# The modulation of two conditioned blocks, moved from matrix products on TensorE to row sums on VectorE

## The chip, the cores and the metric

The kernel runs on one core of one Trainium2 chip. The metric is device time in microseconds, one launch from start to end. Engines are named as the profile names them: PE (TensorE), DVE (VectorE), ACT (ScalarE), POOL (GpSimd), SP (SyncE, which here only issues transfers).

## The reference

A first block (feed-forward, a mixer, feed-forward) works on 256 tokens of width 1024. Then two conditioned layers work on these tokens and on 256 context tokens. All matrices are float32. In each layer a vector of 9 x 1024 numbers, the modulation, is worked out from a condition vector, once for the tokens (`c`) and once for the context (`c_ctx`):

```python
mod = jax.nn.silu(c) @ w_ada[l] + b_ada[l]            # 1024 x 9216, l = 0, 1
modc = jax.nn.silu(c_ctx) @ w_ada[l] + b_ada[l]
def ada_norm(h, g, shift, scale):
    return rms_norm_2(h, g) * (1 + scale) + shift
h = h + HALF * gt1 * swiglu_2(ada_norm(h, g_ffn1[l], sh1, sc1), w1_ffn1[l], w3_ffn1[l], w2_ffn1[l])
u = ada_norm(h, g_mix[l], sh2, sc2)                   # then attention, convolution, Fourier branch
h = h + gt2 * y
h = h + HALF * gt3 * swiglu_2(ada_norm(h, g_ffn2[l], sh3, sc3), w1_ffn2[l], w3_ffn2[l], w2_ffn2[l])
```

A third of the modulation (3 x 1024 numbers) belongs to each of the three parts of a layer. `w_ada` is 37.7 MB per layer, 144 pieces of 512 KB for both.

## The kernel before

**Stages.** In order: f1 (feed-forward, 256 columns), mix1 (gated delta and banded attention), f2 (256 columns), then layer 0 with 512 columns (f10, mix of layer 0, f20) and layer 1 (f11 with 512 columns, mix of layer 1, f21 with 256).

**Weights.** All weights lie in one stream in HBM, cut into units of at most 128 x 1024 numbers (512 KB). SP loads them in order into the ring `w_raw` of NR = 4 slots (line 2201). Before the load of unit u it waits until unit u - 4 is done with: for an ordinary unit until its `w_lo` exists, for a unit of the modulation until its product is over (line 2199). An ordinary unit is split into two halves for fp32r products: ACT writes `w_hi` (line 1520), DVE writes `w_lo` = raw - hi (line 1753), into rings of NH = 3. TensorE then runs three products per 128 x 128 piece (lines 1220 to 1222). So a unit of 8 pieces is 24 matmuls, called a gemm here.

**Order.** `Plan` writes one list of steps, and every engine works through its own steps of that list in order. `with_splits` (line 203) puts the split of a unit AHEAD = 2 units before the step that uses unit u, that is: before the gemm of u stands the split of u + 2.

**Feed-forward** (`ffn`, line 342). For j = 0 to 21: gemm g, gemm u, then the step `ffn_h`: ACT silu (1552), DVE product (1792), ACT high half (1555), DVE low half (1794). One such j is called a turn below. Then for m = 0 to 7 a down gemm of 22 pieces (3 units) and `x_add` (1804), with squares for the next norm.

**Modulation.** A step `ada` is one unit (two pieces of 128 x 512): TensorE multiplies it, with the four columns of `CSIL` as the stationary operand, into a bank of 4 x 512 (line 1259, unsplit float32, two instructions per piece). Four steps make a bank, ACT copies it (1559), four small transposes (1269) turn it and DVE adds the bias (1817, 1819). The 144 steps stand where `FILL` says: beside the norms between stages, beside the attention heads and the delta rule of mix1, beside the latents and heads of the mixes of layers 0 and 1 (42 and 18), and 20 in f11 in split form (1261, 1262). `derive` (line 296) turns a third of the modulation into the factors of the next norm (1824 to 1828).

**Other transfers.** POOL issues the constants of the mixes (lines 2146 to 2185).

The two lines that set when a slot of the raw ring is refilled:

```python
if u >= NR:
    w.wait_ge(*(used(u - NR) if plan.raw_only(u - NR) else at("w_lo", u - NR)))
```

Of the kernel before, what the change touches and what calls it, by code (L numbers as in the profile page):

```python
# [163 lines left out]
class Plan:  # L164


    def __init__(self):
# [4 lines left out]
        self.adas = iter([(l, m, k) for l in range(2) for m in range(18) for k in range(0, 8, 2)])
        self.todo, self.split_ada, self.bank, self.summed, self.rows = 0, False, None, [], []
        self.mod_done, self.count = None, 0
        self.whole()
# [24 lines left out]
    def raw_only(self, u):  # L200
        return self.units[u][2][0][0][0][:3] == "adr"

    def with_splits(self):

        steps, cuts, used, nxt, top = [], [], set(), 0, 0
        self.slot, self.over = {}, {}
        for s in self.steps:
# [4 lines left out]
            else:  # L212
                turns = sorted({wt[0] for wt in s.wts})
            for u in turns:
                if s.wts:
# [1 line left out]
                if s.kind != "ahead":
                    top = max(top, u)
                while nxt < min(u + AHEAD + 1, len(self.units)) and (
                        self.raw_only(nxt) or len(cuts) < NH or cuts[-NH] in used):  # L220
                    if not self.raw_only(nxt):
                        self.slot[nxt] = len(cuts) % NH
                        self.over[nxt] = cuts[-NH] if len(cuts) >= NH else None
                        cuts.append(nxt)
                        steps.append(Step("split", u=nxt))
                    nxt += 1
# [28 lines left out]
    def advance(self):  # L255

        if self.rows:
            l, m, t = self.rows.pop(0)
            b = self.PS.get()
            self.add("ada_col", key=(l, m), b=b, t=t)  # L260
            self.TM.done(t, ("ada_tr", (l, m)))
            self.PS.done(b, ("mod", (l, m)))
            self.mod_done = ("mod", (l, m))
        if self.summed:
            l, m, b = self.summed.pop(0)
            t = self.TM.get()
            self.add("ada_row", key=(l, m), b=b, t=t)
            self.PS.done(b, ("ada_row", (l, m)))
            self.rows.append((l, m, t))

    def fill(self, most=1000):

        while most and self.todo:
            most -= 1
            self.todo -= 1
            l, m, k = next(self.adas)
            self.bank = self.bank or self.PS.get()
            name = f"{'ada' if self.split_ada else 'adr'}{l}"
            wts = self.weights([(name, i, 512 * m, 512) for i in (k, k + 1)])
            self.add("ada", key=(l, m, k), wts=wts, b=self.bank)  # L280
            self.count += 1
            if k == 6:
                self.summed.append((l, m, self.bank))
                self.bank = None

    def due(self, n):
        self.todo += n

    def ada_steps(self, n):
        for _ in range(n):  # L290
            self.due(1)
            self.advance()
            self.fill(1)
            yield

    def derive(self, l, i):
        while any((l_, m) < (l, 6 * (i + 1)) for l_, m, *_ in self.rows + self.summed):
            self.advance()
        assert self.count >= 72 * l + 24 * (i + 1)
        self.add("derive", key=(l, i), need=(self.mod_done,))  # L300

    def stat(self, name, n):
        self.late = None
        return Stat(self, name, n)
# [37 lines left out]
    def ffn(self, p, n, wts, need, gate, old):  # L342
        for j in range(NF):
            if j == 0:
                g, u = self.pair([(p, "g", 0), (p, "u", 0)], wts, n, need)
            else:
                if j <= FILL.get(f"in_{p}", 0):
                    self.split_ada = True
                    self.due(1)
# [20 lines left out]
    def whole(self):  # L370
# [10 lines left out]
        rb = stat.rsqrt(D, between=FILL["mix1"])  # L381
# [14 lines left out]
        rb = stat.rsqrt(D, between=FILL["f10"] // 2)  # L396
# [5 lines left out]
    def block2(self, wts):  # L402
# [4 lines left out]
        for l in range(2):  # L407
# [4 lines left out]
            rb = stat.rsqrt(D, between=FILL["f11"] if l else FILL["f10"] - FILL["f10"] // 2)  # L412
# [1891 lines left out]
```

## Time and profile before

| | |
|---|---|
| time, median of 3 runs (lowest, highest) | 3089.04 us (3087.8, 3096.08) |
| the profiled execution: its time, its span | 3089.18 us, 3087.3 us |
| mean granted clock of TensorE | 0.978 |
| busy: PE, DVE, ACT, POOL | 2929.6, 1464.7, 1073.5, 49.6 us |
| read from HBM | 376.36 MB |
| f10, f20 (512 columns) | 368.4 us each |
| f1, f2 (256 columns) | 184.6, 185.7 us |
| f11 (with 20 split modulation steps) | 388.7 us |
| mix1; mix of layer 0; of layer 1 | 352.6; 573.9; 343.3 us |

The stages are read from the first and last matmul of each. An engine that is busy for a small share of the span can still be the one that a stage waits for; the rows below show the order of events inside a stage. A matmul's duration contains pipelining, so the distance from start to start says more than the duration.

### The profile page before, as it was taken

Reading aid. Unit: us, or ns where it says so; the run is one execution under the profiler, and the core shown is the slowest. Engines: PE = TensorE matmul, PEld = TensorE weight load, DVE = VectorE, ACT = ScalarE, POOL = GpSimd, SP = SyncE. Lnnn points to the kernel's source line nnn. Section 1 sums busy time; section 2 is a strip of 40 time slices with the busy share of each in tenths; the row PEclk is TensorE's granted clock in tenths of the full one; section 3 lists DMA queues with packets and bytes.
Section 4 is the critical chain, followed back from the end, with each engine's and each line's share of the span. In section 5 each row is a group of like instructions: output and inputs, shape, how many; then the busy total and the mean of one; then the engine's idle time right before and its main releaser. Section 6 shows DMA issues by size and latency. Waiting matters only on the chain.

```text
span 3087.3 us, 38316 instructions
## 1 busy us (share of the span) xinstructions
PE 2929.6 (95%) x15892; PEld 2318.7 (75%) x15892; DVE 1464.7 (47%) x2293; ACT 1073.5 (35%) x1630; POOL 49.6 (2%) x49
## 2 busy tenths in 40 slices
PE   8998999999899999988999999999999999879998
PEld 7988457899688885434888788886777866569898
DVE  5556454565433334476333533334444334656664
ACT  5445312444322222233222322223333223335543
POOL 0010022000000000000000000000000000000000
PEclk9999999999999999989999999999999999989999
DMA  6654331555222233422232323323434234215464
GB/s 211 191 206 144 116 103 31 183 196 186 96 96 92 93 97 126 144 78 88 75 96 92 113 90 96 93 94 115 129 124 134 94 125 132 97 51 189 167 194 144
DMA packets 110348, 379.91 MB, mean 123 GB/s; under 512 B 12064, under 2 KB 17440, under 8 KB 109920
## 3 DMA queue, kind: packets, MB, share of 16 engines
q1 hardware_dynamic: 109360, 372.28, 37.4%
q0 software_dynamic: 816, 5.18, 0.5%
q8 instruction: 127, 2.08, 0.3%
q14 instruction: 45, 0.37, 0.0%
HBM read 376.36 MB, written 1.05 MB: 122 GB/s over the span
## 4 chain that ended last, share of the span: by engine, by line
PE 88%; DVE 6%; ACT 3%; DMA 1%; issue 1%; SPq 0%; DVEq 0%; ACTq 0%
PE B L1220 24%; PE B L1221 23%; PE B L1222 23%; PE B L1259 5%; PE B L1457 2%; DMA w_raw<-in_w 1%; DVE w_lo L1753 1%; ACT w_hi L1520 1%; PE B L1235 1%; DVE AC L2012 1%; PE B L1473 1%; PE B L1237 1%; PE B L1236 1%; PE B L1381 1%; PE B L1367 1%
## 5 line engine op out<-in xcount | busy, mean ns | idle before, releaser
L1753 DVE TENSOR_TENSOR w_lo<-w_raw,w_hi 128x1024 fp32r<-128x1024 f32 (+3 forms) x611 | 717.8, 1179 | 851.6 <-ACT w_hi L1520 851.3
L1220 PE MATMUL B<-UH,w_hi 128*128 128x256 f32 (+1 forms) x2896 | 970.5, 335 | 20.4 <-DVE w_lo L1753 18.0
L1221 PE MATMUL B<-UL,w_hi 128*128 128x256 f32 (+1 forms) x2896 | 963.3, 333 | 0.0
L1222 PE MATMUL B<-UH,w_lo 128*128 128x256 f32 (+1 forms) x2896 | 963.0, 333 | 0.0
L1520 ACT ACTIVATE w_hi<-w_raw 128x1024 fp32r<-128x1024 f32 (+3 forms) x611 | 613.1, 1008 | 580.1 <-PE B L1222 531.7
L1220 PEld LDWEIGHTS B<-UH,w_hi 128*128 128x128 f32 x2896 | 547.9, 189 | 95.8 <-issue 21.3
L1221 PEld LDWEIGHTS B<-UL,w_hi 128*128 128x128 f32 x2896 | 547.8, 189 | 62.0 <-issue 1.3
L1222 PEld LDWEIGHTS B<-UH,w_lo 128*128 128x128 f32 x2896 | 547.8, 189 | 61.1
L1220 PE MATMUL B<-HHf,w_hi 128*128 128x256 f32 (+1 forms) x1056 | 354.8, 336 | 0.0
L1221 PE MATMUL B<-HLf,w_hi 128*128 128x256 f32 (+1 forms) x1056 | 354.8, 336 | 0.0
L1222 PE MATMUL B<-HHf,w_lo 128*128 128x256 f32 (+1 forms) x1056 | 354.8, 336 | 0.0
L1259 PE MATMUL B<-w_raw,CSIL 128*4 128x512 f32 x496 | 235.6, 614 | 5.7 <-ACT TMP L1559 5.7
L1555 ACT ACTIVATE HHf<-TMP 128x256 fp32r<-128x256 f32 (+1 forms) x132 | 69.4, 526 | 423.3 <-DVE TMP L1792 423.3
L1220 PEld LDWEIGHTS B<-HHf,w_hi 128*128 128x128 f32 x1056 | 200.4, 190 | 20.8
L1222 PEld LDWEIGHTS B<-HHf,w_lo 128*128 128x128 f32 x1056 | 200.4, 190 | 20.6
L1221 PEld LDWEIGHTS B<-HLf,w_hi 128*128 128x128 f32 x1056 | 200.4, 190 | 20.4
L1792 DVE TENSOR_TENSOR TMP<-TMP,B 128x256 f32<-128x256 f32 (+1 forms) x132 | 73.2, 554 | 238.2 <-PE B L1222 234.6
L1259 PEld LDWEIGHTS B<-w_raw,CSIL 128*4 128x4 f32 x496 | 37.3, 87 | 156.1 <-issue 146.3
L1794 DVE TENSOR_TENSOR HLf<-TMP,HHf 128x256 fp32r<-128x256 f32 (+1 forms) x132 | 73.7, 559 | 78.2 <-ACT HHf L1555 78.2
L2012 DVE SCALAR_TENSOR_TENSOR AC<-VC,PC,AC 128x512 f32<-128x512 f32 (+1 forms) x180 | 99.3, 609 | 0.1
L1525 ACT ACTIVATE TMP<-X 128x256 f32<-128x256 f32 (+1 forms) x77 | 38.3, 512 | 171.0 <-DVE X L1804 136.9
L1457 PE MATMUL B<-QK 96*128 96x512 f32 (+1 forms) x96 | 51.5, 683 | 24.1 <-DVE QK L2064 24.1
(362 smaller groups left out, 2515.7 us busy)
## 6 DMA issues: line engine op xcount, KB each, us to landing
w_raw<-in_w SPq DMA_DIRECT2D x636, 512.0 KB, 3.5
w_raw<-in_w SPq DMA_DIRECT2D x50, 384.0 KB, 3.1
w_raw<-in_w SPq DMA_DIRECT2D x16, 448.0 KB, 4.1
w_raw<-in_w SPq DMA_DIRECT2D x16, 256.0 KB, 2.6
w_raw<-in_w SPq DMA_DIRECT2D x16, 240.0 KB, 2.6
X<-in_x SPq DMA_DIRECT2D x2, 1024.0 KB, 8.7
BW<-in_bias POOLq DMA_DIRECT2D x1, 1536.0 KB, 11.8
K<-in_consts POOLq DMA_DIRECT2D x2, 640.0 KB, 4.8
```

The lines of the kernel that those rows point to most:

```text
L1220: pe.matmul(o, hi, xh, start=i == 0, stop=False)
L1221: pe.matmul(o, hi, xl, start=False, stop=False)
L1222: e = pe.matmul(o, lo, xh, start=False, stop=i == last)
L1259: e = pe.matmul(PS(s.b, 512, 4), CSIL[:, i, :], hi, start=i == 0, stop=i == 7)
L1457: pe.matmul(PS(s.b, nk), QK[:, s.q.i, qs:qs + 128], QK[:, 3 + s.kk.i, k0:k0 + nk], start=True, stop=True).then_inc(*up("soft_s", s.key))
L1520: act.activation(w_hi[:, plan.slot[u], 0:n], w_raw[:, u % NR, 0:n], ACT.Copy).then_inc(*up("w_hi", u))
L1525: act.activation(TM(s.t, s.n), src(s), ACT.Square).then_inc(*up("sq", s.key))
L1555: act.activation(HI[p][:, j, :], TM(s.t, s.n), ACT.Copy).then_inc(*up("hh", s.key))
L1753: dve.tensor_tensor(w_lo[:, plan.slot[u], 0:n], w_raw[:, u % NR, 0:n], w_hi[:, plan.slot[u], 0:n].bitcast(F32), ALU.subtract).then_inc(*up ...
L1792: dve.tensor_tensor(h, h, PS(s.b2, s.n), ALU.mult).then_inc(*up("hm", s.key))
L1794: dve.tensor_tensor(LO[p][:, j, :], h, HI[p][:, j, :].bitcast(F32), ALU.subtract).then_inc(*up("hl", s.key))
L2012: dve.scalar_tensor_tensor(out=AC[:, c], in0=VC[:, c, :, i:i + 256], scalar=col(f"w_dw{l}", 31 * c + i), in1=AC[:, c], op0=ALU.mult, op1=A ...
```

## The change

The modulation is worked out by DVE. The host lays out `w_ada` transposed, so that a unit `adt` is 128 outputs (partitions) by 1024 inputs. Each of 144 steps `ada` is two multiply-and-sum instructions over such a raw unit, one with silu(c), one with silu(c_ctx), which lie as rows repeated over all partitions in `CS` (1 MB, loaded and put through silu at the start). The steps stand only in the feed-forward stages, after `ffn_h` of turns 1 to 21 and after `x_add` of each m: 12, 12, 48, 48 and 24 of them in f1, f2, f10, f20 and f11, spread evenly over the 29 places. All other places of `FILL`, the TensorE products, the copies and transposes go. The bias is added in `derive`. `with_splits` counts only the ordinary units when it looks ahead. The constants of the mixes are issued by ACT and no longer by POOL. NR, NH and AHEAD stay.

```diff
+ADA = {"f1": 12, "f2": 12, "f10": 48, "f20": 48, "f11": 24, "f21": 0}
...
     def with_splits(self):
+        cut = [u for u in range(len(self.units)) if not self.raw_only(u)]
+        place = {u: i for i, u in enumerate(cut)}
...
-                turns = sorted({wt[0] for wt in s.wts})
+                turns = sorted({wt[0] for wt in s.wts} & place.keys())
...
+                at = place[u] if u in place else place[top] + 1
+                while done < min(at + AHEAD + 1, len(cut)) and (done < NH or cut[done - NH] in used):
+                    steps.append(Step("split", u=cut[done]))
+                    done += 1
...
     def gemm(self, key, pieces, n, m=128, x="U", need=(), wts=None):
-        self.advance()
-        self.fill()
...
+    def ada(self, n):
+        for l, b in [next(self.adas) for _ in range(n)]:
+            self.add("ada", key=(l, b), wts=self.weights([(f"adt{l}", b, 0, 1024)]))
+            self.last_ada = (l, b)
...
     def ffn(self, p, n, wts, need, gate, old):
+        turns, share = 0, lambda i: i * ADA[p] // (NF + 7)
...
             self.TM.done(t, ("hl", (p, j)))
+            if j:
+                self.ada(share(turns + 1) - share(turns))
+                turns += 1
...
             stat.add_("X", m, ("x_add", (p, m)))
+            self.ada(share(turns + 1) - share(turns))
+            turns += 1
...
             if k == "load":
+                w.wait_ge(*at("cvec", 0))
+                act.activation(CS[:], CS[:], ACT.Silu).then_inc(*up("cs", 0))
+            elif k == "mix1_load":
+                w.each(s.need)
+                act.dma_start(CN[:], consts[:, 256:2560]).then_inc(*landed("cn", 0))
...
+            if k == "ada":
+                (l, b), u = s.key, s.wts[0][0]
+                raw = w_raw[:, u % NR, :]
+                w.wait_ge(*at(f"w{u % NR}", u))
+                w.wait_ge(*at("cs", 0))
...
+                dve.tensor_tensor_reduce(JUNK[:], raw, CS[:, 0, :], 1.0, 0.0, ALU.mult, ALU.add,
+                                         MOD[:, l, b, 0:1]).then_inc(*up("ada_x", s.key))
+                dve.tensor_tensor_reduce(raw, raw, CS[:, 1, :], 1.0, 0.0, ALU.mult, ALU.add,
+                                         MOD[:, l, b, 1:2]).then_inc(*up("ada", s.key, ("unit", u)))
...
             elif k == "derive":
-                w.each(s.need)
+                mod, bias = MOD[:, l, 24 * i:24 * i + 24, :], col(f"b_ada{l}", 24 * i, 24)
+                w.wait_ge(*at("ada", (l, 24 * i + 23)))
+                dve.tensor_tensor(mod, mod, bias.unsqueeze(2).broadcast_to([128, 24, 2]), ALU.add).then_inc(*up("mod", s.key))
...
         sp.dma_start(C1[:], consts[:, 0:256]).then_inc(*landed("c1", 0))
+        sp.dma_start(CS[:].rearrange("p v k -> p (v k)"), bass.AP(tensor=cvec.tensor, offset=0, ap=[[0, 128], [1, 2048]])).then_inc(
+            *landed("cvec", 0))
```

## Rows read from the trace of the kernel before

**Rows 1.** The page: the chain that ended last, share of the span by line.

```profile
PE B L1220 24%; PE B L1221 23%; PE B L1222 23%; PE B L1259 5%; PE B L1457 2%; DMA w_raw<-in_w 1%; DVE w_lo L1753 1%; ACT w_hi L1520 1%; PE B L1235 1%; DVE AC L2012 1%; PE B L1473 1%; PE B L1237 1%; PE B L1236 1%; PE B L1381 1%; PE B L1367 1%
```

**Rows 2.** Windows: stretch and length, busy time (instructions) by engine, clock, DMA.

```profile
17.40:202.00 184.60, 184.59 (x1584) 184.39 (x1584) 106.87 (x136) 89.52 (x126) 0.00 (x0) 1.00 0.58 187
789.40:1157.80 368.40, 368.39 (x1592) 297.50 (x1592) 130.06 (x160) 104.40 (x134) 0.00 (x0) 1.00 0.29 94
1157.80:1170.40 12.60, 9.23 (x22) 1.86 (x21) 5.57 (x14) 4.62 (x8) 0.90 (x3) 1.00 0.58 188
...
2138.30:2527.00 388.70, 388.66 (x1688) 305.03 (x1688) 153.68 (x188) 125.23 (x158) 0.00 (x0) 1.00 0.37 117
...
2884.00:2892.00 8.00, 1.75 (x5) 0.98 (x5) 5.07 (x11) 5.34 (x9) 0.00 (x0) 0.72 0.57 193
```

**Rows 3.** Chain of waits in 333:396, 396:528, 528:567, 1273:1300, 1300:1450, by line.

```profile
by line: PE B L1259 57.0%; PE B L1309 13.4%; PE B L1326 12.8%; PE B L1317 7.5%; PE B L1291 2.9%; PE B L1269 2.7%; PE B L1339 1.7%; ACT TMP L1559 0.9%; issue 0.8%; PE B L1342 0.7%; ACT PT L1626 0.0%
...
by line: PE B L1381 16.3%; PE B L1367 15.4%; PE B L1374 13.9%; PE B L1259 12.3%; DVE GDN L1955 3.6%; DVE GDN L1953 3.6%; DVE GDN L1957 3.0%; PE B L1396 2.9%; PE B L1351 2.9%; PE B L1355 2.9%; PE B L1412 2.7%; PE B L1342 2.6%; DVE GDN L1959 
...
by line: PE B L1259 22.2%; ACT w_hi L1520 21.4%; issue 20.6%; DMA w_raw<-in_w 12.8%; DVE w_lo L1753 9.9%; DVE X L1810 8.0%; PE B L1419 2.9%; PE B L1246 2.0%; ACT TMP L1559 1.5%; DVE SSB L1760 0.9%; ACT TMP L1525 0.4%; ACTq L1031 0.3%; ACT S
...
by line: PE B L1259 77.7%; PE B L1220 6.6%; PE B L1221 5.1%; PE B L1222 5.1%; PE B L1269 3.7%; PE B L1448 1.6%; PE B L1440 0.9%
...
by line: PE B L1259 20.2%; PE B L1457 18.3%; PE B L1473 10.5%; DVE AC L2012 7.6%; PE B L1464 6.3%; PE B L1220 4.5%; PE B L1221 4.5%; PE B L1222 4.5%; ACT TMP L1697 3.0%; PE B L1448 2.8%; DVE QK L2064 2.3%; DVE TMP L2060 2.1%; DVE w_lo L1753
```

**Rows 4.** Windows over the part of layer 0's mix that holds the convolution's taps.

```profile
1226.00:1450.00 224.00, 198.43 (x692) 92.96 (x690) 139.15 (x302) 59.73 (x136) 0.00 (x0) 0.95 0.35 114
```

**Rows 5.** Timeline of DVE, one turn of f10: start, length [idle before, releaser].

```profile
881.43 0.69 DVE L1792 TENSOR_TENSOR TMP<-TMP,B 128x512 f32<-128x512 f32 x1 [3.29 <-PE B L1222]
882.82 0.69 DVE L1794 TENSOR_TENSOR HLf<-TMP,HHf 128x512 fp32r<-128x512 f32 x1 [0.70 <-ACT HHf L1555]
883.77 1.23 DVE L1753 TENSOR_TENSOR w_lo<-w_raw,w_hi 128x1024 fp32r<-128x1024 f32 x1 [0.26 <-ACT w_hi L1520]
888.11 1.23 DVE L1753 TENSOR_TENSOR w_lo<-w_raw,w_hi 128x1024 fp32r<-128x1024 f32 x1 [3.12 <-ACT w_hi L1520]
892.63 0.69 DVE L1792 TENSOR_TENSOR TMP<-TMP,B 128x512 f32<-128x512 f32 x1 [3.29 <-PE B L1222]
```

**Rows 6.** Timeline of ACT in the same turn.

```profile
882.69 1.04 ACT L1520 ACTIVATE w_hi<-w_raw 128x1024 fp32r<-128x1024 f32 x1
```

**Rows 7.** DMA issues of 790:1160, us to landing; the page's queues, MB and share.

```profile
w_raw<-in_w SPq DMA_DIRECT2D x59, 512.0 KB, 3.3
...
q1 hardware_dynamic: 109360, 372.28, 37.4%
```

**Rows 8.** Timeline of DVE: sums of products in the banded attention of mix1.

```profile
345.40 0.43 DVE L1907 CUSTOM_DVE_ANT_0 TMP<-TMP,CB 128x256 f32<-128x256 f32 x1
345.75 0.08 DVE L1907 DVE_READ_ACCUMULATOR2_ANT SMALL<- 128x1 f32 x1
345.75 0.42 DVE L1907 CUSTOM_DVE_ANT_0 TMP<-TMP,CB 128x256 f32<-128x256 f32 x1
```

**Rows 9.** Timeline of DVE, one turn of f1.

```profile
100.68 0.42 DVE L1792 TENSOR_TENSOR TMP<-TMP,B 128x256 f32<-128x256 f32 x1 [0.41 <-PE B L1222]
101.59 0.43 DVE L1794 TENSOR_TENSOR HLf<-TMP,HHf 128x256 fp32r<-128x256 f32 x1 [0.48 <-ACT HHf L1555]
102.54 1.22 DVE L1753 TENSOR_TENSOR w_lo<-w_raw,w_hi 128x1024 fp32r<-128x1024 f32 x1 [0.52 <-ACT w_hi L1520]
...
106.12 0.42 DVE L1792 TENSOR_TENSOR TMP<-TMP,B 128x256 f32<-128x256 f32 x1 [0.41 <-PE B L1222]
```

**Rows 10.** Timeline of PE, a wait in mix1; and the window after it (clock 0.50).

```profile
223.38 0.55 PE L1220 MATMUL B<-UH,w_hi 128*128 128x256 f32 x1 [3.87 <-DVE w_lo L1753]
...
221.70:228.40 6.70, 5.02 (x23) 5.05 (x24) 5.64 (x9) 1.09 (x3) 0.45 (x1) 0.50 0.50 157
```

**Rows 11.** Chain of waits at the start: start, us, what.

```profile
1.46 6.43 DMA PC<-in_cols
8.68 2.14 ACT TMP L1525 x7
```

More of the change, by code:

```diff
@@ L171, in __init__ @@
         self.nid, self.lastU = 0, None
-        self.adas = iter([(l, m, k) for l in range(2) for m in range(18) for k in range(0, 8, 2)])
-        self.todo, self.split_ada, self.bank, self.summed, self.rows = 0, False, None, [], []
-        self.mod_done, self.count = None, 0
+        self.adas = iter([(l, b) for l in range(2) for b in range(72)])
+        self.last_ada = None
         self.whole()
@@ L200, in raw_only @@
     def raw_only(self, u):
-        return self.units[u][2][0][0][0][:3] == "adr"
+        return self.units[u][2][0][0][0][:3] == "adt"
     def with_splits(self):
-        steps, cuts, used, nxt, top = [], [], set(), 0, 0
-        self.slot, self.over = {}, {}
+        cut = [u for u in range(len(self.units)) if not self.raw_only(u)]
+        place = {u: i for i, u in enumerate(cut)}
+        steps, used, done, top = [], set(), 0, 0
+        self.slot = {u: i % NH for u, i in place.items()}
+        self.over = {u: cut[i - NH] if i >= NH else None for u, i in place.items()}
         for s in self.steps:
@@ L216, in with_splits @@
                     used |= {v for v in turns if v < u}
[L217 to L226, printed above, removed]
+                at = place[u] if u in place else place[top] + 1
+                top = max(top, u) if s.kind != "ahead" else top
+                while done < min(at + AHEAD + 1, len(cut)) and (done < NH or cut[done - NH] in used):
+                    steps.append(Step("split", u=cut[done]))
+                    done += 1
             if s.kind not in ("fetch", "ahead"):
@@ L253, in pair @@
         return b, b2
[L255 to L294, printed above, removed]
-    def derive(self, l, i):
[L297 to L304, printed above, removed]
+    def ada(self, n):
+        for l, b in [next(self.adas) for _ in range(n)]:
+            self.add("ada", key=(l, b), wts=self.weights([(f"adt{l}", b, 0, 1024)]))
+            self.last_ada = (l, b)
+    def derive(self, l, i):
+        assert self.last_ada >= (l, 24 * i + 23)
+        self.add("derive", key=(l, i))
     def norm_to_u(self, name, rb, wait_u):
@@ L380, in whole @@
         wts = self.fetch([("win", k, 128 * j, 128) for k in range(8) for j in range(2)])
-        rb = stat.rsqrt(D, between=FILL["mix1"])
+        rb = stat.rsqrt(D)
         need = self.norm_to_u("mix_norm", rb, self.lastU)
@@ L395, in whole @@
         wts = self.fetch(self.first_of("f10"))
-        rb = stat.rsqrt(D, between=FILL["f10"] // 2)
+        rb = stat.rsqrt(D)
         for k in range(8):
@@ L411, in block2 @@
             self.derive(l, 0)
-            rb = stat.rsqrt(D, between=FILL["f11"] if l else FILL["f10"] - FILL["f10"] // 2)
+            rb = stat.rsqrt(D)
             need = self.ada_to_u(f"n1{l}", l, 0, rb, 512, self.lastU)
@@ L585, in mix1 @@
         tasks += [band(c) for c in range(4)]
-        def later(n):
-            while len(qn) < 8:
-                yield
-            yield from self.ada_steps(n)
-        beside(rounds(tasks, WIDTH1, 1), later(FILL["swa"]))
+        for _ in rounds(tasks, WIDTH1, 1):
+            pass
         first_o = {}
@@ L670, in delta @@
             PS.done(b, ("dl_os", key))
-        beside(rounds([delta(o, d) for o in range(2) for d in range(2)], 4), self.ada_steps(FILL["gdn"] - 5))
-        self.due(5)
+        for _ in rounds([delta(o, d) for o in range(2) for d in range(2)], 4):
+            pass
         def finish(c):
@@ L781, in prep @@
                 q, kk = QR.get(), KR.get()
-                for _ in range(FILL[f"head{l}"]):
-                    self.due(1)
-                    self.advance()
-                    self.fill(1)
-                    yield
                 yield from PS.room(3)
@@ L961, in settle, with rsqrt @@
             self.p.TM.done(self.late, ("sq_add", (self.name, self.i - 1)))
-    def rsqrt(self, count, ring=None, between=0):
+    def rsqrt(self, count, ring=None):
         p = self.p
@@ L1555, in scalar @@
                 act.activation(HI[p][:, j, :], TM(s.t, s.n), ACT.Copy).then_inc(*up("hh", s.key))
-            elif k == "ada_row":
-                w.wait_ge(*at("ada", (*s.key, 6)))
-                w.each(s.t.after)
-                act.activation(TM(s.t, 512, 4), PS(s.b, 512, 4), ACT.Copy).then_inc(*up("ada_row", s.key))
             elif k == "conv_in":
```

111 lines of the change are left out of this document (28 added, 83 removed).

## The prediction

> **What bounds the kernel now.** I read the page's chain first. TensorE products hold nearly all of it, and line 1259, the modulation, is 5% of the span [rows 1]. The windows by stage come next: in the feed-forward stages TensorE never stands still, 184.59 busy in 184.60 us in f1 and 368.39 in 368.40 in f10, while VectorE is busy 106.87 and 130.06 us [rows 2]. By shares alone VectorE has room for the new work. So I looked at how the chain runs in the mixes [rows 3, 4], and then at the order of events in one turn [rows 5, 6, 9] with the loads [rows 7], because every new step also holds a slot of the raw ring until VectorE is through with it.
>
> **What is removed.** Shares of the chain times their stretches give what line 1259 holds on it in the mixes [rows 3]: attention of mix1 0.57 x 63 = 36 us, delta rule 0.123 x 132 = 16, before the out projection 0.222 x 39 = 8.7 with 0.128 x 39 = 5.0 of a refilled raw ring behind it, layer 0 0.777 x 27 = 21 and 0.202 x 150 = 30. Not all of it comes back, for there it fills TensorE while VectorE and ScalarE work.
> - Mix1: of the 36 us of attention I take 27 (six steps at its end stand alone, 11 us; the other 25 us lie between short round trips), of the 16 of the delta rule 10, of 8.7 + 5.0 I take 10, since the out projection still waits for its input. Together 47.
> - Layer 0: from 1226 to 1450 us VectorE is busy 139 of 224 us [rows 4]. If it stays busy at most four fifths of the time, this takes 174 us, 50 less. The taps are dealt out one batch per round of the attention, and rounds that held only modulation vanish, so more taps come alone at the end. I take 45. Bounds are 25 and 56 (the whole chain share, with 3.6 us beside the latents). Layer 1 has 18 steps instead of 42; I take 12.
> - f11 carried 20 split steps: 388.70 against 368.40 us [rows 2], 20 us.
> - The transitions. One with no modulation, 256 columns, takes 8.00 us, one with four steps, 512 columns, 12.60 [rows 2]. After f10 and f20 I take nothing: two new steps stand on VectorE behind the last x_add (4.8 us, below), the third ordinary unit waits for the slot of the first of them, and its split stands ahead of the norm; release, load 3.3, halves 1.04 and 1.23 end at about the old time. Elsewhere: into mix1 2, into f2 6, into f10 8 (six steps were there), into f20 5, into the mix of layer 1 4. Together 25.
> In all 47 + 45 + 12 + 20 + 25 = 149 us less. Bounds: 105 (half of the mixes and transitions, 65, the whole of f11, and the ring's refill and layer 0's far stretch in part, 20) and 185 (every share in full).
>
> **What a new step costs VectorE.** The trace has the same kind of instruction with 256 columns, 0.42 us and 0.35 from start to start, and an ordinary one of 256 columns takes 0.42 too [rows 8, 9]. So 1024 columns take what `w_lo` takes, 1.23 us [rows 5], about 1.2 from start to start, and a step of two takes 2.4 us. As work it is nothing: 48 steps are 115 us beside 130 in 368. The DVE Microarchitecture Reference of the Trainium skill, section "Points that are easy to get wrong", says that a sum over two SBUF sources that aren't bf16 runs at half rate; line 1907 reads two such sources and doesn't [rows 8]; by the rule its pitch would be 0.7, and a step near 4.8 us.
>
> **What a new step costs the ring.** Take a turn of f10. Let 0 be the end of gemm u. VectorE then runs the product and the low half until 2.1 us (881.43 to 883.5), and then `w_lo` of the unit due next [rows 5]. The new steps stand between the two. With a steps, they end at D = 2.1 + 2.4a. With two steps in the next turn the ring of four holds g, u and two steps, so the second new load, g and u can all be issued only at D: the slot before each is the last step's, or stands behind it in SP's queue. A load alone lands 3.3 us after its issue, and further ones 1.5 us apart (372 MB in 37.4% of the span is 322 GB/s, 1.6 us for 512 KB at full use [rows 7]). With two steps, g lands at D + 4.7 and u at D + 6.2; `w_hi` takes 1.04 [rows 6], `w_lo` 1.23 with 0.05 between; u is ready at D + 8.55. In VectorE's order `w_lo` of u stands ahead of the next product, so the next D is 8.55 + 2.1 + 4.8 = 15.45 us later. TensorE needs 11.2 for a turn (881.43 to 892.63 [rows 5]). With one step in the next turn nothing stands ahead of g: 7.05 + 2.1 + 2.4 = 11.55. Of the 21 turns 13 have two steps and 8 have one: 13 x 15.45 + 8 x 11.55 = 293 us against 235, 58 more, less 1 for the start. In the down part (8 turns of 15.35 us) the loads need about 15 us and I take 3. What waits behind the blocked SP queue is the weight of the next turn, and for it TensorE, up to 4.2 us per turn.
> Such gaps cost clock as well: after a wait of 3.87 us the granted clock was 0.50 for 6.7 us [rows 10], which is 1.2 instead of 2.4 GHz. Inside a turn of 15.45 there is room for the 3 us lost, in one of 11.55 there isn't; I take 3 per stage. So f10 and f20 cost 63 each, 126. Bounds for one: 35 (loads land 1 us earlier and 1.0 apart, step 2.2) and 95 (step 2.6, clock low in most turns). The Trainium skill, TensorE: Matmul & The Clock Gate, section "HAM oscillation", describes a loop whose products are shorter than its wait for data and that starts cold each time; here the products are the longer part, so by it too only a part of each turn would be cold.
> f1 and f2: a turn is 5.44 us and has at most one step, 8 in turns and 4 in the down part [rows 9]. D = 1.4 + 2.4 = 3.8. Only u two gemms on waits for the slot: landed 7.1, ready 9.45, due 8.16, so TensorE waits 1.3, and 0.3 to 1 more in the next turn, since VectorE starts its product late. 8 x 1.9 + 4 x 1.4 = 21 each, 42 for both. Bounds 15 and 70. f11: turns of at most one step, 11.55 against 11.2, with four empty turns to recover: 3.
>
> **The rest.** At the start the condition rows (1 MB) stand in SP's queue ahead of the weights, and ACT's silu of 2048 columns (2 x 1.04) waits for them ahead of the squares, which start at 8.68 [rows 11]: 4 us, bounds 0 and 7. The constants move from POOL's queue to ACT's behind the norm: three issues in mix1, hidden beside the norm, 0, bounds -2 and +4. `derive` gains one small instruction, three of six under a longer wait: 0.
>
> **Sum.** 3089.2 (the profiled execution, whose span is 3087.3; the median shown is 3089.0) - 149 + 126 + 42 + 3 + 4 = 3115 us.
>
> **Rivals.**
> 1. The ring stalls as I say, but TensorE is the limit in the mixes, and they give back the whole share: 185 instead of 149, and with the stalls at the lower third (160 instead of 175) 3089 - 185 + 160 = 3064. For it: TensorE is busy 198 of 224 us in [rows 4]. Against: 139 us of VectorE there. It decides where the mixes give back more than the feed-forward stages lose, 175. Chance 0.17.
> 2. The steps hide in the feed-forward stages: the loads come early enough, as VectorE's idle share suggests [rows 2]. Then 3089 - 149 + 4 = 2944. Against: D stands ahead of the load by the order of the units. Chance 0.05.
> 3. The clock falls in each stalled turn of f10 and f20 and TensorE becomes late in turns of one step too: 3 us x 16 turns more, 3163 us. For it [rows 10]. Chance 0.13.
> 4. The sums run at half rate. A step takes 4.8: 13 x 4.8 + 8 x 2.4 = 82 more in each of f10 and f20, some 2.2 us x 24 in f1 and f2: 3332. Against [rows 8]. Chance 0.03.
> My forecast has 0.62.
>
> **How the numbers follow.** A measurement here can't tell less than about 0.3% (9 us) from no change. Between 3080 and 3098 lies about 0.15, taken from the lower side of the forecast and the upper of rival 1. Faster: rivals 1 and 2 less a part, and the lowest of the forecast, 0.2. Slower 0.65. The range is 3065 to 3170: below it rival 2 and half of rival 1, above it rival 4 and a part of rival 3.
>
> **What would show it.** Right: f10 and f20 last about 430 us, TensorE waits there for `w_lo` 3 to 4 us in turns of two steps, ScalarE's `w_hi` waits for the transfer and no longer for TensorE, VectorE's sums take about 1.2 us; f1 and f2 last about 205; layer 0's mix about 530, mix1 about 305; f11 371. Wrong: f10 at 368 (the ring has slack I missed), sums of 2.3 us, or mixes that shorten by less than half of the share of line 1259.

## The result and the profile after

| | before | after |
|---|---|---|
| time, median (lowest, highest), 4 runs each | 3090.53 us (3087.8, 3096.08) | 3105.67 us (3101.86, 3106.81) |
| span of the profiled execution | 3087.3 us | 3100.1 us |
| mean granted clock | 0.978 | 0.946 |

The ratio is 1.0037, interval 1.0023 to 1.0051: slower by 0.4%, which is 11 us by the ratio, 13 by the two profiled executions and 15 by the medians. The forecast was 26 us: the sign came true, about half of the size. The span splits up as follows; a stage begins with the first matmul behind its norm and ends with its last matmul. Forecast terms are those of the prediction, with the transition into f2 and into f20 added to the mix ahead of it.

| stretch | before | after | difference | forecast |
|---|---|---|---|---|
| start of f1 | 17.4 | 21.7 | +4.3 | +4 |
| f1 | 184.6 | 214.5 | +29.9 | +21 |
| to mix1 | 8.7 | 5.8 | -2.9 | -2 |
| mix1, to the start of f2 | 366.7 | 326.8 | -39.9 | -53 |
| f2 | 185.7 | 216.1 | +30.4 | +21 |
| to f10 | 26.3 | 21.2 | -5.1 | -8 |
| f10 | 368.5 | 422.4 | +53.9 | +63 |
| to the mix of layer 0 | 12.6 | 13.5 | +0.9 | 0 |
| mix of layer 0, to the start of f20 | 586.7 | 522.2 | -64.5 | -50 |
| f20 | 368.4 | 426.2 | +57.8 | +63 |
| to f11 | 12.8 | 14.0 | +1.2 | 0 |
| f11 | 388.7 | 367.7 | -21.0 | -17 |
| to the mix of layer 1 | 13.7 | 8.3 | -5.4 | -4 |
| mix of layer 1, to the start of f21 | 351.3 | 318.2 | -33.1 | -12 |
| f21 | 186.0 | 192.0 | +6.0 | 0 |

So 170 us came back (forecast 146) and 182 were paid (forecast 172).

The page of the kernel after: busy time by engine, then the chain that ended last, by engine and by line.

```profile
PE 2747.9 (89%) x15172; PEld 2339.4 (75%) x15172; DVE 1746.8 (56%) x2782; ACT 1043.7 (34%) x1573; POOL 44.7 (1%) x41
...
PE 52%; DVE 20%; DMA 13%; ACT 7%; issue 6%; SPq 1%; DVEq 0%; ACTq 0%
PE B L1155 13%; PE B L1157 13%; PE B L1156 13%; DMA w_raw<-in_w 13%; DVE JUNK L1671 4%; ACT w_hi L1442 4%; DVE w_lo L1678 3%; DVE w_raw L1673 3%; DVE AC L1932 2%; DVE TMP L1717 1%; PE B L1371 1%; ACT HHf L1477 1%; PE B L1170 1%; PE B L1171 1%; PE B L1172 1%
```

Against [rows 1]: before, TensorE held 88% of the chain, now it holds half. The line of the page before:

```profile
PE 88%; DVE 6%; ACT 3%; DMA 1%; issue 1%; SPq 0%; DVEq 0%; ACTq 0%
```

Now transfers hold 13%, VectorE 20%. The same in the page's groups (count, busy time and mean ns of one, then the idle time before them and what ended it):

```profile
L1442 ACT ACTIVATE w_hi<-w_raw 128x1024 fp32r<-128x1024 f32 (+3 forms) x591 | 593.9, 1008 | 997.7 <-DMA w_raw<-in_w 811.8
...
L1673 DVE CUSTOM_DVE_ANT_0 w_raw<-w_raw,CS 128x1024 f32<-128x1024 f32 x144 | 175.6, 1219 | 0.0
L1671 DVE CUSTOM_DVE_ANT_0 JUNK<-w_raw,CS 128x1024 f32<-128x1024 f32 x144 | 175.4, 1218 | 0.0
...
w_raw<-in_w SPq DMA_DIRECT2D x636, 512.0 KB, 3.9
```

288 sums at 1.22 us: the price of the instruction is as forecast, and so is what `w_hi` waits for. The window of f10, with f1 ahead of it (columns as in [rows 2]):

```profile
21.70:236.20 214.50, 197.64 (x1584) 194.08 (x1584) 129.32 (x180) 89.21 (x126) 0.00 (x0) 0.99 0.53 185
806.10:1228.50 422.40, 379.34 (x1584) 306.30 (x1584) 231.19 (x340) 106.04 (x132) 0.00 (x0) 0.96 0.38 136
2204.40:2572.10 367.70, 364.38 (x1584) 298.07 (x1584) 179.90 (x249) 104.81 (x132) 0.00 (x0) 0.99 0.35 123
```

In f10 TensorE was busy 368.39 of 368.40 us [rows 2]; now it stands still 43 us, VectorE is busy 231 of 422, and the granted clock is 0.96. One turn of VectorE in f10, start, length, idle before, as [rows 5]:

```profile
884.89 0.68 DVE L1717 TENSOR_TENSOR TMP<-TMP,B 128x512 f32<-128x512 f32 x1
886.27 0.69 DVE L1719 TENSOR_TENSOR HLf<-TMP,HHf 128x512 fp32r<-128x512 f32 x1 [0.69 <-ACT HHf L1477]
886.88 1.22 DVE L1671 CUSTOM_DVE_ANT_0 JUNK<-w_raw,CS 128x1024 f32<-128x1024 f32 x1
...
888.02 1.22 DVE L1673 CUSTOM_DVE_ANT_0 w_raw<-w_raw,CS 128x1024 f32<-128x1024 f32 x1
...
889.17 1.22 DVE L1671 CUSTOM_DVE_ANT_0 JUNK<-w_raw,CS 128x1024 f32<-128x1024 f32 x1
...
890.31 1.22 DVE L1673 CUSTOM_DVE_ANT_0 w_raw<-w_raw,CS 128x1024 f32<-128x1024 f32 x1
...
896.47 2.45 DVE L1678 TENSOR_TENSOR w_lo<-w_raw,w_hi 128x1024 fp32r<-128x1024 f32 x2 [4.93 <-ACT w_hi L1442]
898.84 0.68 DVE L1717 TENSOR_TENSOR TMP<-TMP,B 128x512 f32<-128x512 f32 x1
...
911.60 0.68 DVE L1717 TENSOR_TENSOR TMP<-TMP,B 128x512 f32<-128x512 f32 x1
...
913.59 1.22 DVE L1671 CUSTOM_DVE_ANT_0 JUNK<-w_raw,CS 128x1024 f32<-128x1024 f32 x1
```

Two steps stand on VectorE from 886.88 to 891.5. Then it waits 4.93 us, not for lack of work but for ScalarE's `w_hi`, and that waits for the transfer (ACT, same turn):

```profile
883.63 0.58 ACT L1474 ACTIVATE TMP<-B 128x512 f32<-128x512 f32 x1
...
895.38 1.06 ACT L1442 ACTIVATE w_hi<-w_raw 128x1024 fp32r<-128x1024 f32 x1 [9.14 <-DMA w_raw<-in_w]
896.61 1.06 ACT L1442 ACTIVATE w_hi<-w_raw 128x1024 fp32r<-128x1024 f32 x1 [0.17 <-DMA w_raw<-in_w]
...
907.93 1.06 ACT L1442 ACTIVATE w_hi<-w_raw 128x1024 fp32r<-128x1024 f32 x1 [7.75 <-DMA w_raw<-in_w]
```

The four loads behind these steps were issued at 889.28, 891.57, 891.94 and 892.42 and landed at 892.51, 895.36, 896.58 and 897.82: 3.2 us for the first; the last three, issued within 0.9 us, landed 1.2 us apart (1.2 to 1.5 in the next two turns). The same wait, over the whole kernel (engine, line, what it waited for: total, times, longest):

```profile
ACT w_hi L1442 <- DMA w_raw<-in_w: 811.8, 209, 10.8
...
ACT w_hi L1442 <- PE B L1157: 160.2, 95, 4.4
PE B L1155 <- DVE w_lo L1678: 131.6, 78, 8.3
```

Before, it was the other way round:

```profile
ACT w_hi L1520 <- PE B L1222: 531.7, 231, 4.4
...
ACT w_hi L1520 <- DMA w_raw<-in_w: 31.5, 19, 4.9
```

### The profile page after: what moved, and what is told of

Its sections match the earlier page's. It is cut to its first block, busy times and chain, and to the rows that moved or that the text cites. A ratio compares the mean times of both kernels' runs of the same rounds, so it can differ in the third digit from the quotient of the medians.

```text
span 3100.1 us, 37377 instructions
## 1 busy us (share of the span) xinstructions
PE 2747.9 (89%) x15172; PEld 2339.4 (75%) x15172; DVE 1746.8 (56%) x2782; ACT 1043.7 (34%) x1573; POOL 44.7 (1%) x41
## 4 chain that ended last, share of the span: by engine, by line
PE 52%; DVE 20%; DMA 13%; ACT 7%; issue 6%; SPq 1%; DVEq 0%; ACTq 0%
PE B L1155 13%; PE B L1157 13%; PE B L1156 13%; DMA w_raw<-in_w 13%; DVE JUNK L1671 4%; ACT w_hi L1442 4%; DVE w_lo L1678 3%; DVE w_raw L1673 3%; DVE AC L1932 2%; DVE TMP L1717 1%; PE B L1371 1%; ACT HHf L1477 1%; PE B L1170 1%; PE B L1171 1%; PE B L1172 1%
## 5 line engine op out<-in xcount | busy, mean ns | idle before, releaser
L1678 DVE TENSOR_TENSOR w_lo<-w_raw,w_hi 128x1024 fp32r<-128x1024 f32 (+3 forms) x591 | 688.1, 1167 | 918.9 <-ACT w_hi L1442 916.5
L1155 PE MATMUL B<-UH,w_hi 128*128 128x256 f32 (+1 forms) x2896 | 992.0, 343 | 123.5 <-DVE w_lo L1678 119.5
L1156 PE MATMUL B<-UL,w_hi 128*128 128x256 f32 (+1 forms) x2896 | 977.9, 338 | 0.0
L1157 PE MATMUL B<-UH,w_lo 128*128 128x256 f32 (+1 forms) x2896 | 976.9, 337 | 0.0
L1442 ACT ACTIVATE w_hi<-w_raw 128x1024 fp32r<-128x1024 f32 (+3 forms) x591 | 593.9, 1008 | 997.7 <-DMA w_raw<-in_w 811.8
L1155 PEld LDWEIGHTS B<-UH,w_hi 128*128 128x128 f32 x2896 | 562.3, 194 | 204.3 <-issue 148.2
L1156 PEld LDWEIGHTS B<-UL,w_hi 128*128 128x128 f32 x2896 | 562.5, 194 | 55.7 <-issue 2.3
L1157 PEld LDWEIGHTS B<-UH,w_lo 128*128 128x128 f32 x2896 | 561.8, 194 | 55.6
L1673 DVE CUSTOM_DVE_ANT_0 w_raw<-w_raw,CS 128x1024 f32<-128x1024 f32 x144 | 175.6, 1219 | 0.0
L1671 DVE CUSTOM_DVE_ANT_0 JUNK<-w_raw,CS 128x1024 f32<-128x1024 f32 x144 | 175.4, 1218 | 0.0
L1170 PE MATMUL B<-UH,w_hi 128*128 128x256 f32 (+1 forms) x144 | 57.6, 400 | 46.1 <-DVE UL L1709 36.9
L1717 DVE TENSOR_TENSOR TMP<-TMP,B 128x256 f32<-128x256 f32 (+1 forms) x132 | 72.5, 549 | 43.7 <-PE B L1157 41.6
```

Source lines behind the costliest of these rows:

```text
L1155: pe.matmul(o, hi, xh, start=i == 0, stop=False)
L1156: pe.matmul(o, hi, xl, start=False, stop=False)
L1157: e = pe.matmul(o, lo, xh, start=False, stop=i == last)
L1170: pe.matmul(o, hi, UH[:, k, 0:s.n], start=k == 0, stop=False)
L1442: act.activation(w_hi[:, plan.slot[u], 0:n], w_raw[:, u % NR, 0:n], ACT.Copy).then_inc(*up("w_hi", u))
L1671: dve.tensor_tensor_reduce(JUNK[:], raw, CS[:, 0, :], 1.0, 0.0, ALU.mult, ALU.add, MOD[:, l, b, 0:1]).then_inc(*up("ada_x", s.key))
```

## The experiments

Times of single runs are good to about 0.3%; the kernels that leave out a part of the modulation's work ran once each. Where a ratio is given, it is to the kernel before on the same chip, whose medians were 3087.3 to 3090.5 us in all groups of runs.

**Is it the ring?** For the 60 us in f10 and f20 my theory was the ring (R in the texts on record): each step holds a slot and so delays the loads behind it. Its rivals were VectorE's own time, which delays the splits, and the transfers, since more bytes cross the same stretch. Six slots or five, with the throwaway output of the sums moved into space that is free in the feed-forward stages, and a smaller scratch for transfers to make room (not shown):

```diff
-NR, NH, AHEAD = 4, 3, 2
+NR, NH, AHEAD = 6, 3, 2
-    CS, JUNK = sb("CS", [128, 2, 1024]), sb("JUNK", [128, 1024])
+    CS = sb("CS", [128, 2, 1024])
...
+            if ADA[p]:
+                if n == 256:
+                    sb("PAD" + p, [128, 11264], F32, st)
+                JK[p] = sb("JUNK" + p, [128, 1024], F32, st)
```

> The changed kernel with six slots in the raw ring instead of four (the scratch output of the sums moves to space that is free in the feed-forward stages). Theory R, the ring: a step keeps its slot until VectorE is through with it, and with six slots the next turn's g waits only for the first step of a turn and lands in time; f10 and f20 fall from 422 and 426 us to 370 to 378, f1 and f2 from 215 to 186 to 192, the whole to about 2945 us. Rival V, VectorE's order: the 4.8 us of sums stand ahead of the halves whatever the ring is; f10 and f20 stay above 410 and the whole above 3080. Rival M, the transfers of these stages interfere: the same as V.

> The same with five slots. Theory R: between the two; in turns of two steps g still stands behind the release of the second step or just before it, so about a half to three quarters of the loss goes: f10 and f20 at 380 to 400 us, f1 and f2 at 190 to 200, the whole at 2970 to 3030. Rivals V and M: no less than 3080.

Six slots: 2924.35 us, ratio 0.9475 (0.9454 to 0.9495), f10 361.7, f20 364.3, f1 191.9, f2 191.5 us. That is below the 370 to 378 us expected for f10 and f20, for a reason that comes further down, the place of the operands. Five: 2995.68 us, 0.9711 (0.9686 to 0.9737), f10 390.8, f20 398.0, f1 195.5. With six slots `w_hi` waits for the transfer less than half as long:

```profile
ACT w_hi L1448 <- DMA w_raw<-in_w: 346.5, 94, 7.7
ACT w_hi L1448 <- PE B L1163: 339.9, 179, 4.7
```

Next, the sums over 8 columns in place of 1024 (slots and loads kept), and the full sums without their loads and slots:

```diff
-                dve.tensor_tensor_reduce(JUNK[:], raw, CS[:, 0, :], 1.0, 0.0, ALU.mult, ALU.add,
+                dve.tensor_tensor_reduce(JUNK[:, 0:8], raw[:, 0:8], CS[:, 0, 0:8], 1.0, 0.0, ALU.mult, ALU.add,
```

```diff
-            self.add("ada", key=(l, b), wts=self.weights([(f"adt{l}", b, 0, 1024)]))
+            self.add("ada", key=(l, b))
...
-                dve.tensor_tensor_reduce(JUNK[:], raw, CS[:, 0, :], 1.0, 0.0, ALU.mult, ALU.add,
+                dve.tensor_tensor_reduce(JUNK[:], CS[:, 1, :], CS[:, 0, :], 1.0, 0.0, ALU.mult, ALU.add,
```

> The changed kernel with sums over 8 columns instead of 1024 (the modulation isn't the reference's); loads, slots, waits and their order stay. Theory R: release comes 2.2 us per step earlier, the loop of two steps is 15 - 4.4 = 10.6 us and under TensorE's 11.2, so f10 is 368 to 374 us and f1 and f2 are 186 to 192. Rival M: f10 stays over 410, since the traffic is the same. V expects the same as R here.

> The changed kernel with the sums of full length over the condition rows alone; the transposed weights are neither loaded nor given a slot (the modulation isn't the reference's). Theory R: VectorE's work alone hides; f10 is 368 to 374 us, f1 and f2 185 to 190. Rival V: f10 stays over 400 and f1 over 205, since the halves stand behind the same sums.

Short sums: 2949.69 us, f10 377.5, f20 371.1, f1 194.2. Full sums without loads: 2912.51 us, f10 360.8, f20 360.9, f1 191.6. So VectorE's 2.4 us per step cost nothing by themselves: with all 288 sums in place f10 runs at full speed when no slot is tied to them. They cost only through the slot that they hold, and most of that goes when the hold is short. Not all: with short sums f10 is still 17 us above the stage without loads, and over the 374 us expected at most; a slot is held until VectorE comes to the step, however short the step is. The bytes aren't it either: with six slots the same bytes cross in a shorter time. The theory of the ring stands, the two others fall.

**Where did more come back than forecast?** The mixes of layers 0 and 1 gave back 97.6 us, forecast 62, the transition into f20 in it. From the kernel before, without any modulation; and with its products 128 columns wide in place of 512 (the units are still loaded and hold slots):

```diff
-            wts = self.weights([(name, i, 512 * m, 512) for i in (k, k + 1)])
-            self.add("ada", key=(l, m, k), wts=wts, b=self.bank)
...
-        self.add("derive", key=(l, i), need=(self.mod_done,))
+        self.add("derive", key=(l, i))
...
+                pool.memset(MOD[:], 0.0).then_inc(*up("mod_zero", 0))
```

```diff
-                        e = pe.matmul(PS(s.b, 512, 4), CSIL[:, i, :], hi, start=i == 0, stop=i == 7)
+                        e = pe.matmul(PS(s.b, 128, 4), CSIL[:, i, :], hi[:, 0:128], start=i == 0, stop=i == 7)
```

> The kernel before with no modulation at all (set to zero): no units, no products, no copies and transposes. It has neither cost, so it gives what the mixes and transitions give back in full, in the layout and with the queues of before. Theory P and L both: layer 1 at 315 to 320 us, layer 0 at 520 to 530, mix1 at 320 to 327, f10, f20 and f11 at 368. If the mixes stay above that, a part of the gain of the changed kernel came from something else in the change (the queue of the constants, the count of the look-ahead).

> The kernel before, with each TensorE product of the modulation 128 columns wide instead of 512 (the modulation isn't the reference's); its units, their loads and their slots stay. Asked is what the mixes gave back: from the start of the mix of layer 1 to f21 the changed kernel took 318 us instead of 351, from the mix of layer 0 to f20 522 instead of 587, from mix1 to f2 327 instead of 367. Theory P: it is TensorE's time, so here most of it comes back too: layer 1 at 323 to 330, layer 0 at 535 to 545, mix1 at 330 to 340. Theory L: it is what the units do to the loads, whose slots they hold until TensorE reaches them; then layer 1 stays above 335 us and its first attention product stays 75 to 86 us behind the start of the mix (before 86, after 58).

Then the opposite: full-width products over a constant, with no units loaded (in f11 they ran unsplit for that, so f11, 408.7 us, is not compared); and the kernel before with six slots.

```diff
-            wts = self.weights([(name, i, 512 * m, 512) for i in (k, k + 1)])
-            self.add("ada", key=(l, m, k), wts=wts, b=self.bank)
+            self.add("ada", key=(l, m, k), b=self.bank)
...
+                    e = pe.matmul(PS(s.b, 512, 4).rearrange('p (a b) -> p a b', a=4), CSIL[:, i, :], C1[:, 0:128].unsqueeze(1).broadcast_to([128, 4, 128]), start=i == 0, stop=i == 7)
```

> The kernel before with TensorE's products of the modulation kept in number and width, but over a constant in SBUF; their units are neither loaded nor given a slot (the modulation isn't the reference's). The complement of the run with narrow products, which left layer 1's mix at 351 us and layer 0's at 577. Theory L, the units' hold on the raw ring and the look-ahead cost the time of these two mixes: layer 1 is 320 to 330 us and layer 0 530 to 550, although TensorE has all its products. Theory P: they stay above 345 and 575. In mix1, where narrow products gave 37 of 40 us, both expect little: 355 to 367.

```diff
-NR, NH, AHEAD = 4, 3, 2
+NR, NH, AHEAD = 6, 3, 2
```

> The kernel before with six slots in the raw ring. Theory L: the modulation's units held slots in the mixes and at the transitions, so layer 1 falls by 10 us or more, the transitions by 2 to 3 us each, and the whole is 3040 to 3060 us. Theory P: the ring was no limit before, 3080 to 3090, and the gain of six slots in the changed kernel is all the repair of its own stall.

| kernel | time | mix1 to f2 | layer 0 to f20 | layer 1 to f21 |
|---|---|---|---|---|
| before | 3090 | 366.7 | 586.7 | 351.3 |
| narrow products, loads kept | 3024.49 | 329.6 | 577.0 | 350.6 |
| full products, no loads | 3076.1 | 359.4 | 577.6 | 345.3 |
| before, six slots | 3080.26 (ratio 0.9971, 0.9957 to 0.9984) | 358.4 | 583.0 | 351.4 |
| no modulation | 2909.6 | 321.4 | 525.2 | 320.8 |
| the change | 3105.67 | 326.8 | 522.2 | 318.2 |

In layers 0 and 1 the changed kernel is as short as the one with no modulation at all: the whole of it came back there. In mix1 the products alone hold it (37 of 45 us). In layers 0 and 1 neither part frees much by itself (10 and 9 of 61 us; 1 and 6 of 30 us), only both together. Both theories on record missed this: with narrow products P expected 323 to 330 us for layer 1 and 535 to 545 for layer 0, and without the loads L expected 320 to 330 and 530 to 550. Six slots in the kernel before came out as P had it, and L had expected 3040 to 3060. The chain by line through layer 1's mix: first the kernel before, then narrow products, then products without loads, then no modulation, then the change.

```profile
by line: PE B L1220 16.8%; PE B L1222 16.1%; PE B L1221 16.0%; PE B L1457 6.0%; PE B L1259 5.4%; PE B L1473 3.5%; DVE AC L2012 3.5%; DVE w_lo L1753 2.4%; ACT w_hi L1520 2.4%; issue 2.3%; PE B L1464 2.0%; DVE UL L1784 1.5%; DVE TMP L1777 1.5
```

```profile
by line: PE B L1220 15.3%; PE B L1221 14.7%; PE B L1222 14.7%; PE B L1457 5.9%; DVE AC L2012 5.5%; issue 4.9%; DVE w_lo L1753 4.7%; ACT w_hi L1520 4.5%; PE B L1473 3.0%; DVE TMP L2097 1.5%; DVE UL L1784 1.5%; DVE TMP L1777 1.5%; DVE SMALL L
```

```profile
by line: PE B L1219 15.2%; PE B L1220 14.5%; PE B L1221 14.5%; PE B L1256 9.7%; PE B L1451 5.9%; issue 4.1%; ACT w_hi L1514 4.0%; PE B L1467 3.5%; DVE AC L2006 2.6%; DVE w_lo L1747 2.2%; PE B L1458 2.2%; DVE UL L1778 1.4%; DVE TMP L1771 1.3
```

```profile
by line: PE B L1213 16.8%; PE B L1215 16.6%; PE B L1214 16.6%; PE B L1450 7.2%; DVE AC L2005 5.6%; PE B L1466 2.9%; DVE w_lo L1746 2.6%; issue 2.3%; ACT w_hi L1513 1.9%; DVE UL L1777 1.6%; DVE TMP L1770 1.6%; DVE TMP L2090 1.5%; PE B L1486 
```

```profile
by line: PE B L1155 14.9%; PE B L1157 14.8%; PE B L1156 14.8%; PE B L1371 6.6%; issue 4.8%; DVE AC L1932 4.3%; ACT w_hi L1442 4.1%; PE B L1387 3.8%; DVE w_lo L1678 3.5%; PE B L1378 1.9%; DVE UL L1709 1.7%; DVE TMP L1702 1.6%; PE B L1407 1.3
```

Line 1259 held 5.4% of 351.3, 19 us. With the products narrow it is gone from the chain, and `w_hi`, `w_lo` and issue stand in its place: 4.5 + 4.7 + 4.9 = 14.1% of 350.6, 49 us, against 7.1%, 25 us, before. Without the loads the products (L1256) hold 9.7% of 345.3, 33 us. Without both, neither is there: 6.8% of 320.8, 22 us, for the splits. So two limits of nearly equal length stood side by side, and each hid the other: that much the four lengths show. One is TensorE's modulation products. What the other is, isn't shown. The chain doesn't settle it, for in the changed kernel `w_hi`, `w_lo` and issue hold 12.4% of 318.2, 39 us, and yet the mix is short. I took it for the way of a slot from release through load and split to the next gemm; against that, six slots free next to nothing in the kernel before (583.0 of 586.7 and 351.4 of 351.3 us), and with narrow products no transfer stands on layer 1's chain. The edit that takes the loads away also takes the units out of the count of the look-ahead, in which each of them uses up one of the two units that a split may run ahead. Late splits are thus a rival that fits as well; neither the new count alone nor narrow products with six slots was run.

**Why did f21 change?** It has no step of the modulation, yet it took 192.0 us and not 186.0, while f11's excess was gone and more. From start to start the products on UH and UL differ, f21 before, f21 after, f10 before, f10 after (PE timelines):

```profile
2950.07 0.28 PE L1222 MATMUL B<-UH,w_lo 128*128 128x256 f32 x1
2950.18 0.28 PE L1220 MATMUL B<-UH,w_hi 128*128 128x256 f32 x1
2950.30 0.28 PE L1221 MATMUL B<-UL,w_hi 128*128 128x256 f32 x1
```

```profile
2960.00 0.28 PE L1155 MATMUL B<-UH,w_hi 128*128 128x256 f32 x1
2960.12 0.28 PE L1156 MATMUL B<-UL,w_hi 128*128 128x256 f32 x1
2960.24 0.28 PE L1157 MATMUL B<-UH,w_lo 128*128 128x256 f32 x1
```

```profile
880.23 0.39 PE L1222 MATMUL B<-UH,w_lo 128*128 128x512 f32 x1
880.46 0.40 PE L1220 MATMUL B<-UH,w_hi 128*128 128x512 f32 x1
880.69 0.39 PE L1221 MATMUL B<-UL,w_hi 128*128 128x512 f32 x1
```

```profile
893.24 0.39 PE L1157 MATMUL B<-UH,w_lo 128*128 128x512 f32 x1
893.47 0.39 PE L1155 MATMUL B<-UH,w_hi 128*128 128x512 f32 x1
893.69 0.39 PE L1156 MATMUL B<-UL,w_hi 128*128 128x512 f32 x1
```

0.113 against 0.120 us for 256 columns, but 0.233 against 0.227 for 512. The change takes 16 columns (64 bytes per partition) of condition vectors out of `PC`, and all that is placed behind moves down. A pad of that size in the changed kernel:

```diff
+    sb("PAD", [128, 16])
```

> The changed kernel with 64 unused bytes per partition behind PC, as the 16 columns that the change took out of it, so that the weight halves lie again as they did. The gemms on UH and UL have 0.120 us from matmul to matmul at 256 columns in f21 (before 0.113), and 0.227 at 512 (before 0.233), though nothing in f21 was changed. Theory A, the place of the operands in SBUF sets it: f21 returns from 192 to 186 us, f1 and f2 lose 6 to 7 us each, f11 grows by 7, f10 and f20 by up to 7 where the ring leaves it to TensorE. Rival S, the order of the splits or the reads of VectorE set it: f21 stays at 192. The whole is within 10 us of the changed kernel either way.

3093.84 us, ratio 1.0015 (1.0003 to 1.0027). f21 186.0, f1 211.6, f2 210.3; f10 428.1, f20 425.6, f11 368.5, and the mixes of layers 0 and 1 at 527.5 and 313.3 us. So the place of the operands set f21's 6 us. Where nothing stalls, the stages without loads against those without modulation show the same: the new place adds 5.6 and 6.9 us to f1 and f2 and takes 7.5, 7.0 and 6.3 off f10, f20 and f11. Where the ring sets the pace, little of that arrives, and there the expectation missed: the pad took 2.9 us off f1 and 5.8 off f2 (6 to 7 expected), put 5.7 on f10, and left f20 and f11 within 1 us (f11 was to grow by 7). The place isn't all that sets the pitch either: with the operands in the old place, f21 of the kernel with no modulation ran at 0.118 us per product and took 190.0 us, and in f1 of the padded kernel gemms at 0.118 and at 0.113 stand in one stage.

**The best version.** With the modulation gone, taps of the convolution stand alone behind layer 0's attention (88 us from its end to the last Fourier product, 59 before). So six slots and more taps per round; and the same with 32 bytes of pad.

```diff
-TAPS, WIDTH, WIDTH1 = (3, 4), 8, 6
+TAPS, WIDTH, WIDTH1 = (5, 6), 8, 6
```

```diff
+    sb("PAD", [128, 8])
```

> The changed kernel with six slots, and with the convolution's taps dealt out in batches of 5 (layer 0) and 6 (layer 1) instead of 3 and 4. The forecast's account of the mix of layer 0: rounds that held only modulation are gone, so taps are left over and run alone behind the attention, and from the last attention product to the end of the Fourier branch it is 88 us where it was 59. If that is right, larger batches bring this back to 60 to 70 us while the attention grows by less; the whole falls from 2924 to 2900 to 2915 us. Rival: VectorE bounds the attention as well, and what leaves the tail comes back in it; 2920 to 2930.

> The same with 32 unused bytes per partition behind PC. 64 bytes there turned 0.120 us per matmul of 256 columns on UH and UL into 0.113, and 0.227 at 512 columns into 0.233. If the distance modulo 64 bytes sets it, 32 bytes give a third value or swap one of the two alone; expected is one of the two known pairs (f21 192 or 186 us, f11 361 or 368), with the whole within 10 us of the run without the pad. f21 at 186 together with f11 at 361 would be the better of both, 2885 to 2900.

The taps: 2911.8 us, 0.942 (0.9404 to 0.9436), as expected, and the fastest of the kernels that do the whole work. The tail is 61 us, but the attention grew, and layer 0 gained 11 us (513.6), layer 1 lost 2 (320.1). With the pad 2922.86 us, 0.9456 (0.9438 to 0.9474): f10 368.9, f20 367.9, f11 368.2, f1 190.4, f21 190.6. It has the slow pitch for 512 columns and one in between for 256 (0.118 us, which the old place has shown too), not the better of both. It missed.

## Where the prediction was right and where it was wrong

The sign was right; of the size, 26 us, about half came. The step that failed is what the mixes of layers 0 and 1 give back.

**The step on VectorE** (2.4 us): right, 1.22 us per sum, 1.14 from start to start. Rival 4, the half rate, is out. What the prediction cited from the Trainium skill (Vector Engine (DVE) Microarchitecture Reference, "Points that are easy to get wrong") on two SBUF sources that aren't bf16 doesn't show here; the page states it for one instruction layout, and the profile doesn't tell whether this instruction has it.

**The ring** (63 us in f10, 21 in f1): right, and it is the reason of the result. The order was as written: VectorE's steps, release, load, halves, gemm. In f10, by turn, it is less even than forecast: after two steps and ahead of two a turn takes 14.9 to 15.5 us (forecast 15.45), two ahead of one 13.4 to 14.0 (11.55), one ahead of two 12.8 to 13.3 (15.45); the three together 41.8 against 42.45. Loads issued together were 1.2 to 1.5 apart, where 1.5 was taken. Against the stages without the loads, which have the new place of the operands, f10 and f20 cost 62 and 65 us (360.8, 360.9) and f1 and f2 23 each (191.6, 192.8).

**The clock** (3 us a stage): a wrong way of counting with little harm. TensorE's products took 379.3 us in f10, 18 more than the 361 without a stall, at a granted clock of 0.96. The clock was at 0.50 in six stretches, 34 us in all, of which half, 17 us, is lost. But these 18 us lie inside turns whose length the ring sets, so they add nothing to it: in f10 and f20 VectorE's product (L1717) had no idle time ahead of it from the third turn on, so it waited for nothing there, TensorE included. Rival 3, where the clock makes TensorE the limit, is out. The prediction also misread [rows 10]: the 6.7 us at 0.50 began 1.7 us before the wait of 3.87 us was over, so only 5 us of them lay behind it.

**What went wrong**: "Layer 1 has 18 steps instead of 42; I take 12" failed, and with it "I take 45" for layer 0. Layer 1 gave 33.1 us and layer 0 64.5, with 5 for the transition. Layer 0's came from the chain's share of line 1259 and from how busy VectorE was in one window, layer 1's was layer 0's scaled by the steps and cut further; the chain's share was the upper bound in the forecast. It is no bound. It tells which of two limits came last, not what frees when one goes: in layer 1 the share was 19 us, the products alone were worth 1, the loads of the units alone 6, and both together 30; in layer 0 they were worth 10, 9 and 61. The change took both out of the mixes. The trace before had `w_hi` and `w_lo` on the chain between the products, and I didn't ask what made them late; what it was stays open (above). Rival 1 stated as much in sign ("they give back the whole share"); of its two halves the first came nearly true, 170 us of its 185, and the cheaper stalls did not, 182 against 160. In mix1 I took too much (53, measured 40), for there the share of [rows 3] was overlap.

**Start, f11, transitions**: +4.3, -21.0, -11.3 against +4, -17, -14. Right within a few us. In f11 the 24 steps cost 7 us in the new place of the operands (367.7 against 360.7 with six slots) and 1 in the old (368.5 with the pad against 367.9 with no modulation), where 3 was taken.

**Not in the prediction at all**: the operands' place. By the pad it cost +6 us in f21, +6 in f2 and +3 in f1, and gave back 6 in f10 alone. The pad moves the whole kernel by 12 us, as much as the whole result: with it the change is at 1.0015. So that the sign came clear of the noise owes much to a term that nobody had forecast.

**Range and chances**: 3105.67 lies inside 3065 to 3170, and the side forecast with 0.65 came. The forecast was a small difference of two large sums: 26 = 172 - 146, and the trace has 182 - 170. An error of 24 us in one sum is a sixth of it, and as much as the whole forecast; the 10 us more that were paid, 6 of them in f21, hid a part of it.

**Open**: whether the new count of `with_splits` alone, in the kernel before, changes the mixes; it wasn't tried. So it isn't known what the second limit in the mixes of layers 0 and 1 was. What in a place of SBUF sets the pitch of a matmul isn't known either, only that 64 bytes change it, and that something else changes it too.

## What to carry to other kernels

Work moved to an idle engine is paid where it holds a shared buffer, not where it computes: here 48 steps of 2.4 us on VectorE were free, and the slots they held cost 60 us per stage; two more slots turned 1.004 into 0.9475, where they turned the kernel before only into 0.9971. Count the turn of the ring first, from release to the next use, and give it slots enough before judging the move. And a line's share of the chain is no upper limit of what removing it brings, if the same edit also removes the limit next to it; look for what else the removed work holds.

## What the hardware showed that was not expected

The pitch of fp32r matmuls changed with the place of their operands: 0.113 or 0.120 us for 256 columns, 0.227 or 0.233 us for 512, the better one of each in opposite kernels, with 64 bytes between them; with 32 bytes the whole stage of 256 columns took 190.6 us, between 186.0 and 192.0. The pads moved the weights' halves and UH and UL together, so which of them matters isn't shown, and 0.118 us stands in the old place too. The down products, on HHf and HLf, took 63.5 us a stage (256) and 119.8 or 119.9 (512) in every stage that had no stall, in either place. And of loads of 512 KB issued one right behind the other, the later ones landed, in three turns of f10, 1.2 to 1.5 us apart, some 430 GB/s at 1.22 us, where the mean of the span had let me expect 1.5.
